# Rows of a second product behind the feed-forward tiles, head roots ahead of the crosswise copies, and three bank sets for the projections of a two-block transformer kernel

## What is computed

```python
mod_l = (silu(c) @ w_ada[layer] + b_ada[layer])          # 6 x 1024 values, also for c_ctx
h = rms_norm(x) * (1 + scale) + shift
q = apply_rope(rms_norm(split_heads(h @ w_q), gain), cos, sin)   # differential and grouped-query attention
k = apply_rope(rms_norm(split_heads(h @ w_k), gain), cos, sin)
v = split_heads(h @ w_v)
f = (silu(conv(h @ w_gate)) * (h @ w_up)) @ w_down       # feed-forward, hidden width 2816
```

## Time and profile before

| | us |
|---|---|
| median of 3 executions | 2717.91 (2716.37 to 2718.04) |
| the profiled execution's own time | 2716.32 |
| its span (first to last instruction) | 2714.5 |
| TensorE busy / VectorE busy | 2528.6 / 1520.3 |
| ScalarE busy / GpSimd busy | 931.6 / 832.0 |

### The profile page before, as it was taken

The page is one execution under the profiler, slowest core; times in us unless marked ns, Lnnn a source line. Parts: engine busy times, 40 slices in busy tenths (PEclk is TensorE's granted clock), DMA queues, the critical chain, the costliest instruction groups (busy, mean ns, idle before and its releaser), DMA issues.

```text
span 2714.5 us, 37430 instructions
## 1 busy us (share of the span) xinstructions
PE 2528.6 (93%) x14490; PEld 2072.8 (76%) x14490; DVE 1520.3 (56%) x2136; ACT 931.6 (34%) x1410; POOL 832.0 (31%) x445
## 2 busy tenths in 40 slices
PE   7899898999998887988899999999998997999998
PEld 5577887778887766866687888888876765788887
DVE  2366755666676846476545654654775466533242
ACT  3366123222224535335423222122255421433232
POOL 2333012544441221223222332222222320344443
PEclk9899988999998989999999999999998998999999
DMA  4212002444441100112013332322311020232222
GB/s 165 78 55 78 3 32 93 162 163 162 155 170 48 55 32 1 53 47 50 9 55 117 132 110 96 120 101 95 121 56 53 32 78 8 86 109 100 94 99 79
DMA packets 78422, 227.43 MB, mean 84 GB/s; under 512 B 21440, under 2 KB 23488, under 8 KB 77770
## 3 DMA queue, kind: packets, MB, share of 16 engines
q1 hardware_dynamic: 64056, 172.92, 18.7%
q10 hardware_dynamic: 14226, 52.54, 5.6%
HBM read 223.32 MB, written 2.12 MB: 83 GB/s over the span
## 4 chain that ended last, share of the span: by engine, by line
PE 78%; DVE 11%; issue 5%; ACT 3%; POOL 1%; DMA 0%; DVEq 0%; ACTq 0%; POOLq 0%
PE ps L271 19%; PE ps L272 19%; PE ps L273 19%; PE ps L737 3%; PE ps L752 3%; PE ps L768 2%; DVE rstd L647 2%; POOL w_lo L2310 1%; DVE ada_place L1009 1%; PE ps L411 1%; PE ps L363 1%; PE ps L2141 1%; PE ps L342 1%; PE ps L343 1%; PE ps L764 1%
## 5 line engine op out<-in xcount | busy, mean ns | idle before, releaser
L2310 POOL TENSOR_TENSOR w_lo<-ring,w_hi 128x1024 fp32r<-128x1024 f32 x293 | 712.2, 2431 | 1471.1 <-ACT w_hi L264 950.9
L271 PE MATMUL ps<-act_hi,w_hi 128*128 128x512 f32 x2280 | 845.2, 371 | 28.9 <-POOL w_lo L2310 12.4
L273 PE MATMUL ps<-act_hi,w_lo 128*128 128x512 f32 x2280 | 831.4, 365 | 0.0
L271 PEld LDWEIGHTS ps<-act_hi,w_hi 128*128 128x128 f32 x2280 | 431.6, 189 | 113.8 <-issue 20.5
L272 PE MATMUL ps<-act_lo_ffn,w_hi 128*128 128x512 f32 (+1 forms) x1408 | 514.7, 366 | 0.0
L273 PEld LDWEIGHTS ps<-act_hi,w_lo 128*128 128x128 f32 x2280 | 430.3, 189 | 72.5
L264 ACT CAST w_hi<-ring 128x1024 fp32r<-128x1024 f32 (+1 forms) x167 | 174.1, 1043 | 710.0 <-PE ps L273 607.5
L1009 DVE SCALAR_TENSOR_TENSOR ada_place<-ada_place 128x1024 f32<-128x1024 f32 x192 | 330.4, 1721 | 34.4 <-DMA ada_place<-in_w_ada 9.9
L272 PEld LDWEIGHTS ps<-act_lo_ffn,w_hi 128*128 128x128 f32 x1408 | 266.4, 189 | 42.2 <-issue 0.7
L1079 ACT CAST w_hi<-ring 128x1024 fp32r<-128x1024 f32 (+1 forms) x132 | 137.6, 1043 | 455.2 <-PE ps L273 455.2
L271 PE MATMUL ps<-hidden_hi,w_hi 128*128 128x512 f32 x704 | 256.6, 364 | 3.5 <-POOL w_lo L2310 1.9
(11 more groups left out here) (366 smaller groups left out, 3324.4 us busy)
## 6 DMA issues: line engine op xcount, KB each, us to landing
ring<-in_w_ffn SPq DMA_DIRECT2D x204, 512.0 KB, 3.2
ada_place<-in_w_ada ACTq DMA_DIRECT2D x96, 512.0 KB, 3.2
ring<-in_w_gdn SPq DMA_DIRECT2D x16, 512.0 KB, 3.2
ring<-in_w_hy SPq DMA_DIRECT2D x12, 512.0 KB, 3.2
ring<-in_w_dil_qk SPq DMA_DIRECT2D x8, 512.0 KB, 6.4
ring<-in_w_out SPq DMA_DIRECT2D x8, 512.0 KB, 3.2
ring<-in_w_diff_qk SPq DMA_DIRECT2D x8, 512.0 KB, 3.7
ring<-in_w_na_qk SPq DMA_DIRECT2D x8, 512.0 KB, 3.2
```

Source lines behind the costliest of these rows:

```text
L271: pe.matmul(out, w[0], x[0], start=start, stop=False)
L273: return pe.matmul(out, w[1], x[0], start=False, stop=stop)
L2310: pool.tensor_tensor(k.w_lo[:, a % SPLITS, :], k.ring[:, a % SLOTS, :], k.w_hi[:, a % SPLITS, :].bitcast(F32), ALU.subtract).then_inc(k.lo ...
```

## The change

```diff
-def values_unit(k, pe, name, lo, blocks, width, u):
+def values_unit(k, pe, name, lo, blocks, width, u, units, tiles=None):
...
-    for b in range(blocks):
+    order = range(blocks)
+    if tiles is not None:
+        evac, evacuated, n = tiles
+        holder = [max(i for i in range(n) if i % 3 == b // 2) for b in range(blocks)]
+        order = sorted(order, key=lambda b: holder[b])
+    for b in order:
+        if tiles is not None and u == 0:
+            pe.wait_ge(evac, evacuated + holder[b] + 1)
...
-    last.then_inc(k.unit_done, 1)
+        if b == order[-1]:
+            last.then_inc(k.unit_done, 1)
+        elif u == units - 1:
+            last.then_inc(k.sem("values_made"), 1)
+
+
+VALUES = {"w_dil_v": (0, 4, None), "w_diff_v": (3, 6, 8), "w_na_v": (8, 6, 8)}
+
+
+def values_out(k, e, name, dst, copy, first):
+
+    before, blocks, n = VALUES[name]
+    order = list(range(blocks))
+    if n is not None:
+        order.sort(key=lambda b: max(i for i in range(n) if i % 3 == b // 2))
+    for at in range(first, blocks, 2):
+        b = order[at]
+        if at < blocks - 1:
+            e.eng.wait_ge(k.sem("values_made"), before + at + 1)
+        else:
+            e.eng.wait_ge(k.unit_done, FIRST[name] + 4)
+        link(e, copy(dst[:, b, :], k.bank(b, HALF)))
...
-    link(v, v.eng.tensor_tensor(x, x, xs, ALU.add))
+    v.eng.tensor_tensor(x, x, xs, ALU.add).then_inc(k.sem("head_rotated"), 1)
...
-                    if i >= 2:
-                        pe.wait_ge(self.evac, self.e + i - 1)
+                    if i >= 3:
+                        pe.wait_ge(self.evac, self.e + i - 2)
...
-                    unit_products(k, pe, i % 2, u, k.h_hi, lo, DT, widths)
+                    unit_products(k, pe, i % 3, u, k.h_hi, lo, DT, widths)
...
-                if i == n:
-                    pe.wait_ge(self.evac, self.e + n)
-                values_unit(k, pe, self.values, lo, T // P, self.width, i - n)
+                values_unit(k, pe, self.values, lo, T // P, self.width, i - n, self.units, (self.evac, self.e, n))
...
-            if i < n:
-                if self.jobs[i][5] is not None:
-                    if i >= 2:
-                        s.eng.wait_ge(self.normed, self.b + i - 1)
-                    swap_halves(s, swapped(k, i), src[:, 0:S])
-                s.eng.copy(back(x), blocks(src)).then_inc(self.evac, 1)
+
+        def keep(i):
...
+            if self.jobs[i][5] is not None:
+                if i >= 2:
+                    s.eng.wait_ge(k.sem("head_rotated"), self.r + i - 1)
+                swap_halves(s, swapped(k, i), src[:, 0:S])
...
+            s.eng.copy(x, src).then_inc(self.evac, 1)
...
-
-        s.eng.wait_ge(k.unit_done, FIRST[self.values] + self.units)
-        for b in range(3, 6):
-            link(s, s.eng.copy(self.dst[:, b, :], k.bank(b, self.width)))
+            if i < n:
+                keep(i)
+
+        values_out(k, s, self.values, self.dst, s.eng.copy, 1)
...
-        v.eng.wait_ge(k.unit_done, FIRST[self.values] + self.units)
-        for b in range(3):
-            link(v, v.eng.tensor_copy(self.dst[:, b, :], k.bank(b, self.width)))
+        values_out(k, v, self.values, self.dst, v.eng.tensor_copy, 0)
...
-    def step(self, c):
-
-        return CHUNKS[c][0] + DT * c
+    def step(self, c, a):
+
+        return CHUNKS[c][0] + DT * c + a + 2 if c else a - 1
+
+    def steps(self, c, j):
+
+        if c:
+            return [CHUNKS[c][0] + DT * c + CHUNKS[c][1] + j + 2]
+        n = CHUNKS[0][1] - 1 + j + min((j + 1) // 2, 3)
+        return [n, n + 1] if j in (0, 2, 4) else [n]
...
         self.ada_load(s, 0)
-        self.ada_load(s, 1)
+
+    def ada_rows(self, s):
...
-                if static and c == 0 and a == 0:
-                    f.ada_load(s, 2)
...
-                f.ada_load(s, f.step(c) + a + 3, it)
+                if begun:
+                    f.ada_rows(s)
+                else:
+                    f.ada_load(s, f.step(c, a) + 1, it)
...
-            f.ada_load(s, f.step(c) + nm + j + 3)
+            for row in f.steps(c, j):
+                f.ada_load(s, row + 1)
...
-                f.ada_tile(v, f.step(c) + a + 2, it)
+                if static and c == 0:
+                    if a == 1 and f.ada is not None:
+                        v.eng.wait_ge(k.ada_rows_ready, f.ada + 1)
+                        f.ada_tile(v, 0)
+                else:
+                    f.ada_tile(v, f.step(c, a), it)
...
-        if c == 0 and f.ada is not None:
-            v.eng.wait_ge(k.ada_rows_ready, f.ada + 1)
-            f.ada_tile(v, 0)
-            f.ada_tile(v, 1)
...
-    return 4 if t % 2 == 0 else 0
+    return (4, 0, 2, 4)[t]
...
-            pe.wait_ge(evac, (1, 3, 4)[t - 1])
+            pe.wait_ge(evac, (1, 2, 3)[t - 1])
```

More of the change, by code:

```diff
@@ L534, in rope_vector, with __init__ @@
     link(v, v.eng.scalar_tensor_tensor(xs, xs, gain_swap, k.const("sin", 0, S), ALU.mult, ALU.mult))
-    link(v, v.eng.tensor_tensor(x, x, xs, ALU.add))
+    v.eng.tensor_tensor(x, x, xs, ALU.add).then_inc(k.sem("head_rotated"), 1)
 class Projection:
-    def __init__(self, k, name, tiles, values, units, width, dst, before, evacuated, turned, jobs):
+    def __init__(self, k, name, tiles, values, units, width, dst, before, evacuated, rotated, turned, jobs):
         self.k, self.name, self.tiles, self.values, self.units = k, name, tiles, values, units
-        self.width, self.dst, self.b, self.e, self.jobs = width, dst, before, evacuated, jobs
+        self.width, self.dst, self.b, self.e, self.r, self.jobs = width, dst, before, evacuated, rotated, jobs
         self.evac, self.backward = k.sem("head_evac"), turned
@@ L598, in square @@
             size = x.shape[-1]
-            src = k.ps[:, 1024 * (i % 2):1024 * (i % 2) + size] if i < n else x
+            src = k.ps[:, 1024 * (i % 3):1024 * (i % 3) + size] if i < n else x
             if i >= 2:
@@ L985, in ada_load @@
         k, at = self.k, ADA * self.ada + n
-        if at >= 2:
+        if at >= 2 or n < 2 and not isinstance(it, int):
             s.eng.wait_ge(k.ada_used, it * 2 + (at - 1))
@@ L996, in ada_begin @@
         self.ada_load(s, 0)
-        self.ada_load(s, 1)
+    def ada_rows(self, s):
+        if self.ada is None:
+            return
+        k = self.k
         s.eng.wait_ge(k.ada_rows, 16 * (self.ada + 1))
@@ L1125, in ffn_vector, with up @@
         u = f.u0 + f.off(c)
-        def up(it):
+        def up(it, static):
             for a in range(2):
@@ L1183, in ffn_vector @@
             v.eng.wait_ge(f.added, f.outs + DT * c + j + 1)
-            f.ada_tile(v, f.step(c) + nm + j + 2)
+            for row in f.steps(c, j):
+                f.ada_tile(v, row)
     f.ada_end(v)
@@ L1322 @@
 GQA = 28
+GQA_ROTATED = 8
 def gqa_bank(t):
-    return 4 if t % 2 == 0 else 0
+    return (4, 0, 2, 4)[t]
 def gqa_project_tensor(k, pe):
@@ L1406, in gqa_project_scalar @@
         s.eng.activation(k.sq[:, (t + 1) % 2, 0:S], src, ACT.Square).then_inc(squares, 1)
[L1407 to L1410, removed]
         if t == 0:
@@ L1416, in gqa_project_scalar @@
             root(t - 1)
+        if t >= 1:
+            s.eng.wait_ge(k.sem("head_rotated"), GQA_ROTATED + t)
+        swap_halves(s, swapped(k, t + 1), src)
+        s.eng.copy(q[:, t, 0:S], src).then_inc(evac, 1)
         if t == 1:
@@ L1433, in gqa_project_vector, with invert @@
         .then_inc(normed, 1)
-    for t in range(4):
-        v.eng.wait_ge(evac, 3 + t)
-        rope_vector(k, v, q[:, t, 0:S], swapped(k, t + 1), k.par("gqa_q"), k.par("gqa_q_swap"))
+    def invert(t):
         v.eng.wait_ge(rooted, GQA + 2 + t)
@@ L1440, in gqa_project_vector, with rotate, scale @@
             .then_inc(k.sem("gqa_inverted"), 1)
+    def rotate(t):
+        v.eng.wait_ge(evac, 3 + t)
+        rope_vector(k, v, q[:, t, 0:S], swapped(k, t + 1), k.par("gqa_q"), k.par("gqa_q_swap"))
+    def scale(t):
         v.eng.wait_ge(k.sem("gqa_spread"), t + 1)
+        v.eng.wait_ge(k.sem("head_rotated"), GQA_ROTATED + 2 + t)
         v.eng.tensor_tensor(q[:, t, 0:S], q[:, t, 0:S], k.bank(7), ALU.mult).then_inc(normed, 1)
+    rotate(0)
+    for t in range(1, 4):
+        invert(t - 1)
+        rotate(t)
+        scale(t - 1)
+    invert(3)
+    scale(3)
     v.eng.wait_ge(normed, GQA + 5)
@@ L1524, in start_scalar @@
     s.eng.wait_ge(k.sem("lam_exps"), 1)
-def values_vector(k, v, name, units, dst, width, blocks):
-    v.eng.wait_ge(k.unit_done, FIRST[name] + units)
-    for b in range(blocks):
-        link(v, v.eng.tensor_copy(dst[:, b, :], k.bank(b, width)))
 def dil_project_tensor(k, pe):
@@ L1546, in dil_project_tensor @@
     for u in range(4):
-        values_unit(k, pe, "w_dil_v", k.lo1, 4, HALF, u)
+        values_unit(k, pe, "w_dil_v", k.lo1, 4, HALF, u, 4)
 def dil_project_vector(k, v):
@@ L1554, in dil_project_vector @@
     v.eng.wait_ge(k.sem("dil_lines_kept"), 1)
[L1555 removed]
+    values_out(k, v, "w_dil_v", dil_views(k)[2], v.eng.tensor_copy, 0)
```

(1 more changed line is left out.)

14 lines of the change are left out of this document (9 added, 5 removed).

## The result

| | before | changed |
|---|---|---|
| median | 2717.29 us (2716.37 to 2718.04, 4 runs) | 2682.95 us (2680.66 to 2686.31, 4 runs) |
| span of the profiled execution | 2714.5 us | 2678.9 us |
| mean granted clock | 0.957 | 0.964 |

The account below looks back on a forecast made before the run. TensorE, busy for 93% of the span, was taken as the bound, so only its idle and lower-clock time could go. Terms summed to -30.4 us against 2716.3: 2685.9, plus 1.6 for the median, forecast 2687.5 us, range 2680 to 2694.

Parts of the forecast that it names:

- First network, start: First feed-forward's start: TensorE's gap goes (-6.5 us) and the clock gives back 2.3; term -8.8 us.
- Chunk 0's down units: First feed-forward: three more rows on an already full VectorE cost +7.0 us, bounds nothing to 13.7.
- The count of stretched products: Chunk 0's down units: lowerings stay one a unit, so extra rows meet no more of them; hence 7.0, not 13.7.
- the full-price rival: Both networks: each extra row gets a stretched product and VectorE's lateness reaches TensorE; 13.7 + 4.2, 2698 us; chance 0.14.
- Second network: Second feed-forward: start gives -7.4 us, gap and clock; paired rows in the down units cost +0.4, bounds 0 and 4.2.
- Diff: Diff projection: waits of 7.7 and 1.62 us go, plus 3.2 of clock; term -12.5, bounds -9 and -14.
- so I count no clock there: TensorE's gaps of 1.62 and 1.32 us: first matmul takes 0.50 us, not 0.79, so no clock loss counted.
- VectorE has about 8.4 us of work a tile: Diff projection: with the root ahead and copies waiting for the rotation alone, VectorE's work is about 8.4 us; TensorE paces.
- Na, grouped-query, dilated: Three projections: wait before na values goes, -1.3 us; grouped-query root and scale waits, -7.2; dilated copies shared, -0.6.
- late conditioning rows: First network's start, rival: no slack, a transfer 3 us later costs 3 and part of 2.3; 2692 us; chance 0.07.
- the slow case: Down units, rival: clock stays at 1.2 GHz, TensorE slower than VectorE, up to 74 us lost; 2754 us; chance 0.03.
- the gaps between the pairs: First network's chunk 0: down units in pairs with gaps of 3 to 5 us, chunk 1 starting some 7 us later.

Follow-up runs that it names:

- after_again: The changed kernel unaltered, run again on one chip beside the kernel before; median 2681.41 us, ratio to before 0.9874.
- four_places: The changed kernel with two more places for rows in chunk 0's down units, transfers issued two rows ahead there; 2675.43 us, ratio to before 0.9856.
- rows_in_up: The changed kernel with two rows a hidden tile in chunk 0's up (tiles 1 to 5), six behind down units; 2667.77 us, ratio to before 0.9828.
- banks_only: The kernel before with three bank sets and the new order of value blocks in both projections; 2705.20 us, ratio to before 0.9962.
- values_together: The changed kernel, but value banks are copied only when the last value unit is all done; 2680.21 us, ratio to before 0.9874.
- gqa_old_vector: The kernel before with the grouped-query part, but VectorE's old order (rotate, invert, scale each tile); 2702.39 us, ratio to before 0.9968.

## Why the prediction held

2682.95 us against 2687.5 forecast, inside the likeliest case's own range. The sum over the touched stages, -30.9 against -30.4, is closer than its terms are: the first network cost 2.6 us more than forecast and the other stages gave 3.1 more. That they cancel is luck. The terms, against the table above:

- *First network, start*: -8.8 against 73.0 - 81.7 = -8.7. The gap and the clock behind it went as reckoned.
- *Chunk 0's down units*: +7.0 against +9.5. The step that failed is "Each row more costs at least two products of 1.22 and their reads, 2.5 us: 7.6 for three. Against that, half a microsecond of ScalarE's waiting may overlap." Up to the seventh copy it is 11.1: 7.6 for the rows, 4.3 for late transfers, less 0.8 of stretching (`after_again` has 10.7 with transfers of 2.8 and slightly more stretching than before). A row's transfer is issued when the row two before it is used; behind a pair that leaves too little time, and I had looked at what VectorE does, not at when its rows land. Then 1.6 come back, which I had not counted, because chunk 1's first unit no longer runs at 1.2 GHz (574.02 - 561.15 = 12.9 us from the gap to the product before, 574.13 - 562.84 = 11.3 after). `four_places` shows that the late transfers are not by themselves the price: with them gone, other waits filled the time. What sets the 9.5 is therefore open; `rows_in_up` shows that it goes with the rows themselves.
- *The count of stretched products*, on which the full-price rival hung, held. From first to seventh copy the changed kernel has nine rows; 42.9 less 9 x 2.54 for rows, 4.3 for copies and 4.3 for transfers leaves 11.4 us of stretching; before, 31.8 less 15.2 and 4.3 leaves 12.3 for six rows. One by one, seven of twelve products are longer than 1.5 us before, six of eighteen now and seven of eighteen in `after_again`, with seven lowerings each time. More rows met no more lowerings. That agrees with the lock in the Trainium skill (SBUF — State Buffer, section "SBUF: two separate sides") as I had read it.
- *Second network*: -7.4 and +0.4, measured -7.3 together. Pairs run there without idle time on VectorE, but TensorE shows no gap of 0.5 us before the network's closing norm: a down unit takes it 6.3 us, and VectorE's steps, 7.3 to 8.0 with a pair and 4.6 with one row, average to about that.
- *Diff*: -12.5 against -13.8. All of the clock's cost went, and the value stretch runs at full clock. The reading "so I count no clock there" came out right for a reason that is none: the granted clock is 1.00 behind both gaps (881 to 885, 1176 to 1182), but a first matmul of 0.50 does not tell that, as the gap of 2.67 in the earlier trace rows and the 2.26 in `banks_only` show. "VectorE has about 8.4 us of work a tile" was too low as the row shows it: it is never idle, since its product with the root takes 2.10 us. The same product takes 0.69 in the grouped-query stage (L1479), so 1.4 of each tile's 9.69 us is stretching, and TensorE still paces. I had said that VectorE would be seen to wait for roots; it is not.
- *Na, grouped-query, dilated*: -1.3, -7.2, -0.6 against -1.6, -8.3, -0.7. The grouped-query term was near without its mechanism: it adds up VectorE's waits (2.9 and 4.3) and has no clock in it, and 3.6 of the 8.3 are clock. Copying the value banks singly was costed at nothing, and `values_together` shows nothing.
- *Rivals*: late conditioning rows cost nothing (ScalarE waited 0.28 us for them); the slow case's long low clock in the down units did not come; it fell twice for part of a unit (0.53 and 0.50 as above), with a mean of 0.93 from 516 to 563.
- *Signs*: the gaps between the pairs are 2.76, 3.96 and 3.56 us, about the 3 to 5 foretold. From the first down unit to chunk 1 TensorE takes 46.6 us instead of 35.5 (516.25 to 562.84, 525.70 to 561.15), so chunk 1 starts 11 us later and not 7.

The touched stages explain 31 of the 33 to 34 us between the medians. The last 2 or 3 are in stages that vary by as much between executions of one program, and no run settles them.

## What to carry to other kernels

Extra work for an engine belongs where that engine idles, and its idle time in each stage is read before a place is chosen: three more rows cost 9.5 us in the down units, and 9.0 when they were moved to the last of them, while five rows moved from there to the hidden tiles, where VectorE idled 4 us a tile, made four tiles 1.0 us longer in all and the network 14.4 us shorter. When work on an engine is doubled at one place, look at the transfers that feed it and at what is queued behind the engine that issues them. To judge parts of a change worth a few us each, compare stage lengths in traces and measure parts in each other's presence: in the diff projection two parts added up to 0.1 us, in the na projection one of them alone was a loss of 2.4. Stages that a kernel leaves alone set the noise, and they differ too: the diff projection took 127.0 us in `gqa_old_vector`, whose diff leaves it alone, and 128.8 before. And a shorter wait on TensorE is not the whole gain: read its busy time in the stage for what the clock gives back.

## What the hardware showed that I had not expected

Stages without any difference in the program came out at different lengths: one norm at 27.9 to 28.3 us in nine traces and at 31.0 in three, with mean granted clocks of 0.64 and 0.57 in the two shown, and one attention at 114.1 to 118.5 us. And idle times on TensorE of 2.76, 3.96, 3.56 and 2.37 us in the changed kernel's down units cost no more than the 4.9 us of short waits and the one of 6.48 in `four_places`. The lower clock came in both, only at another place: behind the second and third wait in the changed kernel, within down units where VectorE sets the pace, and in chunk 1's first unit in `four_places`, where two units then took 13.4 us instead of 11.3.
